# The closing sums of the backward recurrence move from VectorE to GpSimd

## The reference, cut to what matters

```python
h_fwd = rg_lru_direction(xc, ..., False)
h_bwd = rg_lru_direction(xc, ..., True)
lru = (h_fwd + h_bwd) * gelu(y_gate)
branch_lru = lru @ w_proj_lru
```

## Time and profile before

| what | us |
|---|---|
| runs, median (lowest to highest of 3) | 1541.71 (1541.62 to 1542.18) |
| profiled execution, span of its instructions | 1540.0 |
| TensorE busy in it | 1521.3 |
| VectorE busy | 854.5 |
| ScalarE busy | 472.3 |
| GpSimd busy | 22.7 |

### The profile page before, as it was taken

The page is one execution under the profiler, slowest core; times in us unless marked ns, Lnnn a source line. Parts: engine busy times, 40 slices in busy tenths (PEclk is TensorE's granted clock), DMA queues, the critical chain, the costliest instruction groups (busy, mean ns, idle before and its releaser), DMA issues.

```text
span 1540.0 us, 28457 instructions
## 1 busy us (share of the span) xinstructions
PE 1521.3 (99%) x12084; PEld 888.8 (58%) x12084; DVE 854.5 (55%) x1885; ACT 472.3 (31%) x693; POOL 22.7 (1%) x37
## 2 busy tenths in 40 slices
PE   9999999999999999999999999999999999999997
PEld 6887888888888878844334334334334344343342
DVE  7778776888787776653335336145145334352262
ACT  5698745444457976410000000000000000000001
POOL 0000000000000000000000000000000000000000
PEclk9999999999999999999999999999999999999999
DMA  9444365555543444599999999999999999999993
GB/s 382 176 163 165 112 244 205 192 191 189 194 176 139 157 147 162 198 370 414 404 410 426 410 416 422 406 421 417 408 426 418 407 426 412 412 424 407 423 425 126
DMA packets 68068, 478.13 MB, mean 310 GB/s; under 512 B 7585, under 2 KB 7841, under 8 KB 11874
## 3 DMA queue, kind: packets, MB, share of 16 engines
q1 hardware_dynamic: 64192, 460.35, 74.7%
q0 software_dynamic: 3456, 15.72, 2.7%
q10 hardware_dynamic: 290, 0.19, 0.0%
HBM read 471.38 MB, written 4.85 MB: 309 GB/s over the span
## 4 chain that ended last, share of the span: by engine, by line
PE 87%; ACT 6%; DVE 4%; issue 1%; DMA 1%; SPq 0%; DVEq 0%; ACTq 0%
PE bank L1403 27%; PE turn L1418 12%; PE mid L1403 11%; PE bank L1126 7%; PE bank L1132 7%; PE bank L1135 7%; PE turn L1430 6%; PE mid L1126 2%; PE mid L1132 2%; PE mid L1135 2%; ACT w_hi L558 1%; DVE w_lo L565 1%; PE mid L1238 1%; ACT root L917 1%; ACT rg L929 1%
## 5 line engine op out<-in xcount | busy, mean ns | idle before, releaser
L1403 PE MATMUL bank<-wide,gT 128*32 128x512 f32 (+1 forms) x3952 | 423.7, 565 | 0.0
L1403 PEld LDWEIGHTS bank<-wide,gT 128*32 128x32 f32 x3952 | 155.8, 110 | 244.4 <-issue 237.8
L565 DVE TENSOR_TENSOR w_lo<-raw,w_hi 128x1024 fp32r<-128x1024 f32 x202 | 244.2, 1222 | 92.7 <-ACT w_hi L558 90.4
L558 ACT ACTIVATE w_hi<-raw 128x1024 fp32r<-128x1024 f32 (+1 forms) x202 | 210.2, 1053 | 100.9 <-PE bank L1135 65.8
L2002 DVE STREAM_TRANSPOSE hT<-eh 32x128 f32<-32x128 f32 (+1 forms) x768 | 220.0, 286 | 24.1
L1418 PE MATMUL turn<-wide,hT 128*32 128x512 f32 x1792 | 215.4, 592 | 0.0
L1403 PE MATMUL mid<-wide,gT 128*32 128x256 f32 (+1 forms) x2048 | 192.1, 486 | 0.0
L1046 ACT ACTIVATE eh<-bank 128x512 f32<-128x512 f32 (+1 forms) x32 | 17.4, 544 | 534.6 <-PE bank L1403 306.2
L1126 PE MATMUL bank<-w_hi,a_hi 128*128 128x512 f32 (+1 forms) x608 | 164.6, 394 | 0.8 <-ACT a_hi L783 0.8
L1135 PE MATMUL bank<-w_lo,a_hi 128*128 128x512 f32 (+1 forms) x608 | 157.1, 382 | 2.2 <-DVE w_lo L565 2.2
L1132 PE MATMUL bank<-w_hi,a_lo 128*128 128x512 f32 (+1 forms) x608 | 157.4, 382 | 0.0
(11 more groups left out here) (258 smaller groups left out, 1195.0 us busy)
## 6 DMA issues: line engine op xcount, KB each, us to landing
wide<-in_stream SPq DMA_DIRECT2D x330, 1024.0 KB, 8.0
raw<-in_stream SPq DMA_DIRECT2D x106, 1024.0 KB, 4.8
wg<-in_gates POOLq DMA_DIRECT2D x2, 2048.0 KB, 10.9
table<-y_rows POOLq DMA_DIRECT2D x7, 384.0 KB, 7.7
gain<-in_norms POOLq DMA_DIRECT2D x4, 512.0 KB, 7.3
x<-in_x SPq DMA_DIRECT2D x2, 512.0 KB, 6.1
raw<-in_stream SPq DMA_DIRECT2D x2, 512.0 KB, 6.6
tokens<-xs POOLq DMA_DIRECT2D x1, 1024.0 KB, 5.8
```

The lines of the kernel that those rows point to most:

```text
L558: nc.scalar.activation(w_hi[:, h % H, 0:n], raw[:, part % R, lo:lo + n], ACT.Copy).then_inc(hi_ready, 1)
L565: nc.vector.tensor_tensor(w_lo[:, h % H, :], raw[:, part % R, lo:lo + HALF], w_hi[:, h % H, :].bitcast(F32), ALU.subtract).then_inc(lo_rea ...
L1403: ins = nc.tensor.matmul(bank_[strip(s_), 0:w], gT[:, kt, strip(t_)], w_c, start=kt == 0, stop=kt == KT - 1)
```

## The change

The sum after the backward scans is issued by GpSimd, which does nothing else in those places. GpSimd waits for the forward scans of these channels (`scanned`) and for the four backward scans (a new semaphore, `back_scanned`), adds, and counts `scanned` up by 4 as VectorE did. VectorE goes on from the scans to its next step with no wait.

```diff
@@ gpsimd, in its walk over STEPS
+                elif s[0] == "ls" and s[2] == 1:
+                    _, L, d, hf = s
+                    n4 = slice(4 * hf, 4 * hf + 4)
+                    pool.wait_ge(scanned, scans_done(L, 0, 1) + 4 * hf)
+                    pool.wait_ge(back_scanned, 8 * L + 4 * hf + 4)
+                    nc.gpsimd.tensor_tensor(xT[:, n4, 0:T], xT[:, n4, 0:T], root[:, :, :],
+                                            ALU.add).then_inc(scanned, 4)
@@ vector
                             nc.vector.tensor_tensor_scan(root[:, q, back], rg[:, n, back], ig[:, n, back],
-                                                         0.0, ALU.mult, ALU.add).then_inc(chain, 1)
-                            links[0] += 1
-                    if d == 1:
-                        dve.wait_ge(chain, links[0])
-                        nc.vector.tensor_tensor(xT[:, n4, 0:T], xT[:, n4, 0:T], root[:, :, :],
-                                                ALU.add).then_inc(scanned, 4)
+                                                         0.0, ALU.mult, ALU.add).then_inc(back_scanned, 1)
```

More of the change, by code:

```diff
@@ L476, in build @@
         scanned = sem("scanned")
+        back_scanned = sem("second_direction_scanned")
         rope_s = sem("rope_parts")
```

## The result

The changed kernel takes 1548.49 us (median of 5 runs, 1547.07 to 1549.75) against 1542.18 for the one before (1541.62 to 1542.43): 6.3 us or 0.42% slower, ratio 1.0042 with a 95% interval of 1.0031 to 1.0053. The profiled execution is the quickest of the five, 1547.07 us with a span of 1545.3, 5.3 us over the span of before. The work is further behind than the span tells: ScalarE's first `xn` of the closing norm begins 6.27 us later.

A forecast was written before the change was run, and what follows sets the result against it. The kernel was taken as bound by TensorE (99% busy). The first sum ends late, shifting ScalarE's `la` by 2.2 us per layer: 2 x 2.2 = 4.4, 1541.7 + 4.4 = 1546.1 us, 0.29% slower; whole range 1543.8 to 1548.9.

The forecast's parts named there:

- GpSimd waits for both: First sum starts only after both `w_lo`, at 124.66: shift 3.33, 7.0 us in all, 1548.7 us; chance 0.20.
- TensorE's wait for `w_lo` vanishes, and the gain is not kept: At 124.92 us TensorE gains 1.09 us, but its later wait for ScalarE's `gy` grows by the same 1.09.
- The hop: From VectorE's scans to GpSimd's sum 0.20 us, from the sum to ScalarE's `la` 0.03 us.
- The add: GpSimd's 128x1024 sum takes 2.4 us, with 0.95 and 2.85 as ends.
- The meeting: Beside VectorE's two `w_lo`, GpSimd starts after the first, at 123.53, 0.93 us late; the second `w_lo` is held back.
- starting at 123.5 and 2.4 us long: Sign expected in the changed kernel's trace: when GpSimd's first sum starts and how long it lasts.
- The second sum costs nothing: Each layer's second sum is covered by `qkT`'s wait for TensorE; behind all four `w_lo` it costs 0.2 us per layer.
- TensorE waits at half 37: Late `w_hi` of half 37, at 133.2, makes TensorE wait there already, as part of the same 2.2 us delay.
- VectorE queues nothing behind a wait any more: Under costs nothing: after the change VectorE has no work standing behind a wait; no size given.
- The clock: Rival: longer TensorE idle stretches slow matmuls afterwards, some us per layer, 1550 us or more; chance 0.06.
- Not slower: Rival: add at the memset's pace without waiting, shift -0.18, 1541.3 us; decided at an add of 1.13 us; chance 0.05.

The follow-up runs named there:

- second profile: The changed kernel run again with nothing edited, for a second look and its spread: 1548.24 us, ratio 1.0042 (1.0027 to 1.0057) to the kernel before.
- third profile: The changed kernel run once more with nothing edited, one execution, for four more of GpSimd's records: 1548.48 us.

## Why the prediction was right, point by point

The forecast was 1546.1 us, 0.29% slower, in a range of 1543.8 to 1548.9; measured were 1548.49 and 0.42%. The direction and the mechanism hold: the sum ends later, and ScalarE's block carries that to TensorE. The size is less well met. The measured time lies above the forecast's own part of the range (1545.3 to 1547.0) and 0.2 us below the rival in which GpSimd waits for both `w_lo` (1548.7). Part of that nearness is luck: the rival happens in some places only, the add was taken too long, and the second sum too cheap.

- *TensorE's wait for `w_lo` vanishes, and the gain is not kept.* Right: no wait at 123.88, and 1.38 us before L1257 on top of the new ones.
- *The hop.* 0.18 us (scans end at 122.55, the record starts at 122.73), taken as 0.20; to ScalarE 0.03, as taken.
- *The add.* 2.17 us alone, taken as 2.4, by bounds of 0.95 and 2.85; the ratio to VectorE's 1.23 is 1.76. Behind the first `w_lo`, which ended at 122.47 + 1.23 = 123.70, it is done in 2.02 us (at 125.72). That is 0.4 less than taken, and the whole difference between the forecast's shift of 2.2 and the measured 1.84 in the case that it describes.
- *The meeting.* GpSimd behind the first `w_lo`, the second held: shown, 3.0 us in the record and 4.33 for the pair. The record begins when GpSimd asks (122.73) and holds the standing still, so the sign "starting at 123.5 and 2.4 us long" did not come as such. The rival "GpSimd waits for both" is shown as well, in 3 of 8 first places (those of the run with the first sums only counted in), with a shift of 2.99 (127.07 less 0.32 against 123.76) where 3.33 was reckoned. In the changed kernel's three profiled executions the shifts are 1.84, 2.99 and 1.85 in layer 0 and 2.19, 2.19 and 3.34 in layer 1, which hold the unexplained 0.35 us. The mean is 2.4 per layer, 4.8 for both, where the forecast had 2.2 and 4.4.
- *The second sum costs nothing.* This step was mis-sized. It fell behind the whole run of four `w_lo` in 5 of 6, and then it costs 1.04 us, not the 0.2 that I had for that case. I had followed `qkT` only to TensorE's next use of it (L1264); the loss came out later, at the transposes of the probabilities (166.37), where VectorE had yet to read a `turn` bank (`att_lo`, 165.94 to 166.22) and was late because its `w_lo` waits for the `w_hi` that ScalarE does behind `qkT`. Where the record was 3.00 (layer 0 of the second profile) the first and third product with `qkT` are 16.48 us apart, as before, and nothing is lost. On average 5/6 x 1.04 = 0.87 us per layer, 1.7 for both. That with the 4.8 makes 6.5 us, which is the mean of the three executions' delays and agrees with the 6.3 measured (4.8 to 8.2).
- *Where the delay shows.* "TensorE waits at half 37" was wrong. It waits one step earlier, at the transposes of `ty(1)`, for VectorE's half of the `y` evacuation (L1589), which stands in VectorE's list behind the `w_lo` of half 36, which waits for ScalarE's `w_hi`, which stands behind `la`. The sentence "VectorE queues nothing behind a wait any more" had missed this: it queues behind ScalarE. The time at which TensorE passes L1257 is not changed by it.
- *The clock.* Named as a rival with 0.06, at some us per layer. The clock falls in some executions at waits of 2.3 to 3.9 us, but it cost the changed kernel nothing in any of its three profiles: in the first and third it does not fall in the recurrences. In layer 0 of the second one half 36 took 4.43 us (132.54 to 136.97) against 2.83 (131.24 to 134.07), and TensorE then found `gy` just ready, so the 1.6 us was hidden in what would have been the second wait. Only in layer 0 of the run with the first sums only was it longer than that wait, and cost 0.9 us. The other terms make up the 6.3 us without it.
- *Not slower.* Would have needed an add of 1.13 us; it is 2.17.

What was argued from the chain of waits alone, that the first sum hurts through `root`'s single buffer, is shown by the variants with `root` set free: the same four sums on GpSimd then cost nothing that can be measured (1536.94 us against 1537.45 with VectorE's). It is not the only way in which the sums hurt: the second one's 1.7 us come through `qkT`. That way was not tested with `root` set free, since all four records of that profile are 3.0 us long.

## What to carry to other kernels

Before work is moved to a slower engine, ask who waits for its result, not how busy the old engine is: here VectorE was 55% busy, but the moved add lay on a chain from the scans over ScalarE to TensorE, and 0.9 us more of duration and the meeting with `w_lo` outweighed the 1.3 us that VectorE saved. The wait itself was the thing to remove, and a buffer that already existed did it (4.6 us, against 6.3 us lost by the move). GpSimd's work in SBUF should not be placed where VectorE begins an unbroken run of instructions with two SBUF inputs, for it may have to wait for the whole run; `tensor_scalar` from SBUF held it up as well.

## What the runs showed of the hardware that was not expected

- An unbroken run of VectorE instructions with two SBUF inputs let a GpSimd add in behind its first instruction or behind its last, in no case between: 3.0 us records against 4.1 (run of two), 5.3 (three) and 6.4 us (four). A request 1.12 us after the first of four began (each 1.2 us long) already waited for all. Why requests 0.26 us after it fell either way in the kernel is open.
- One SBUF input can be enough for a meeting: beside four `tensor_scalar` of 128x1024 from SBUF the add's record is 2.53 us. With one of two inputs in PSUM it stays 2.17.
- The record of a held instruction includes its standing still, on both engines: 3.06 in place of 2.17 on GpSimd, and 2.0 us more on VectorE. So the meeting can be read off durations alone.
- TensorE's granted clock fell to 0.50 at waits of 3.88 and 2.33 us in the second profile of the changed kernel and at waits of 3.85 and 2.33 us in the run with the first sums only, and stayed at 1.00 behind one of 3.84 us in the third profile and of 2.32 us in the first.
